# Gathering the tokens of a mixture-of-experts layer already transposed, four groups at a time

## The reference

```python
gu = jnp.einsum("td,edf->tef", h, w_expert_gu)
act = jax.nn.silu(gu[..., :EXPERT_DIM]) * gu[..., EXPERT_DIM:] * combine[..., None]
routed = jnp.einsum("tef,efd->td", act, w_expert_down)
...
x = x + gate_f * rmsnorm(f, g_post_ffn)
```

## Time and profile before

| | |
|---|---|
| median of 3 runs | 794.63 us (790.98 to 795.26) |
| the profiled execution | 798.48 us, of which the span from first to last instruction is 796.3 us |
| PE busy | 740.0 us (93% of the span) |
| DVE busy | 421.1 us (53%) |
| ACT busy | 226.0 us (28%) |
| expert weights | 64 loads of 2048 KB and 64 of 1024 KB |
| all DMA | 256.05 MB, mean 322 GB/s |

### The profile page before, as it was taken

How to read it: one execution, slowest core, us unless ns; L and a number is a source line. 1 busy time by engine, 2 the same in 40 slices (tenths; PEclk the granted TensorE clock), 3 DMA queues, 4 the chain that set the end, 5 groups by cost and what they waited for, 6 DMA issues and landing times.

```text
span 796.3 us, 12271 instructions
## 1 busy us (share of the span) xinstructions
PE 740.0 (93%) x4613; PEld 450.0 (57%) x4613; DVE 421.1 (53%) x1003; ACT 226.0 (28%) x383; POOL 85.0 (11%) x48
## 2 busy tenths in 40 slices
PE   1589999799999999999999999999999999999984
PEld 1489887687755455554544555544545555544442
DVE  3278999384366655544444445444444445544344
ACT  3225332662351122222222222222222222222132
POOL 2235554303210000000000000000000000000000
PEclk9989999989999999999999999999999999999997
DMA  9996565804595389999999999999999999999611
GB/s 322 374 363 227 212 217 206 319 1 159 143 421 204 105 323 347 367 428 426 395 430 416 357 407 427 391 424 428 377 424 419 391 428 397 362 431 422 238 55 81
DMA packets 47263, 256.05 MB, mean 322 GB/s; under 512 B 6240, under 2 KB 8896, under 8 KB 30432
## 3 DMA queue, kind: packets, MB, share of 16 engines
q1 hardware_dynamic: 39360, 247.47, 77.8%
q0 software_dynamic: 1664, 4.35, 1.8%
q10 hardware_dynamic: 6176, 3.40, 1.6%
HBM read 253.07 MB, written 2.13 MB: 320 GB/s over the span
## 4 chain that ended last, share of the span: by engine, by line
PE 76%; DMA 11%; DVE 9%; ACT 2%; issue 1%; SPq 0%; ACTq 0%; DVEq 0%
PE psum L1917 25%; PE psum L1946 10%; PE psum L1872 9%; PE psum L1889 8%; DMA w_gu<-in_w_expert_gu 7%; PE psum L498 4%; PE psum L500 3%; PE psum L499 3%; DVE psum L1026 3%; PE psum L1881 3%; PE psum L1799 3%; DMA w_gu<-in_w_in 2%; DMA w_gu<-in_w_ada 2%; PE psum L1816 1%; PE psum L1863 1%
## 5 line engine op out<-in xcount | busy, mean ns | idle before, releaser
L1917 PE MATMUL psum<-w_gu,hgT 128*32 128x512 f32 (+1 forms) x1344 | 199.7, 599 | 5.3 <-DMA w_gu<-in_w_expert_gu 4.6
L1416 DVE TENSOR_TENSOR f_acc<-f_acc,psum 128x512 f32<-128x512 f32 x168 | 115.5, 688 | 50.1 <-PE psum L1889 50.0
L1917 PEld LDWEIGHTS psum<-w_gu,hgT 128*32 128x32 f32 (+1 forms) x1344 | 61.3, 120 | 141.0 <-issue 140.1
L1946 PE MATMUL psum<-w_dn,actT 128*32 128x512 f32 (+1 forms) x672 | 102.1, 596 | 0.0
L1407 DVE TENSOR_TENSOR y_lo<-psum,y_hi 128x1024 fp32r<-128x1024 f32 x28 | 34.3, 1225 | 106.7 <-ACT y_hi L893 106.7
L1872 PE MATMUL psum<-h_hi,onehot 128*128 128x512 f32 x174 | 71.1, 409 | 0.0
L493 POOL TENSOR_TENSOR w_lo<-w_gu,w_hi 128x2048 fp32r<-128x2048 f32 x14 | 64.4, 4600 | 62.9 <-ACT w_hi L652 62.9
L1889 PE MATMUL psum<-y_hi,onehotT 128*128 128x512 f32 x168 | 70.4, 419 | 0.0
L1399 DVE SCALAR_TENSOR_TENSOR act<-sil,wsl,psum 128x256 f32<-128x256 f32 x28 | 19.0, 679 | 94.6 <-ACT sil L888 94.6
L1872 PE MATMUL psum<-h_lo,onehot 128*128 128x512 f32 x174 | 68.1, 391 | 0.0
L1889 PE MATMUL psum<-y_lo,onehotT 128*128 128x512 f32 x168 | 66.2, 394 | 0.0
(11 more groups left out here) (292 smaller groups left out, 952.7 us busy)
## 6 DMA issues: line engine op xcount, KB each, us to landing
w_gu<-in_w_expert_gu SPq DMA_DIRECT2D x64, 2048.0 KB, 13.3
w_dn<-in_w_expert_down SPq DMA_DIRECT2D x64, 1024.0 KB, 10.4
w_gu<-in_w_ada SPq DMA_DIRECT2D x12, 2048.0 KB, 16.1
w_gu<-in_w_in SPq DMA_DIRECT2D x4, 2048.0 KB, 8.5
w_gu<-in_w_out SPq DMA_DIRECT2D x2, 2048.0 KB, 10.1
bc<-mod_rows POOLq DMA_DIRECT2D x6, 512.0 KB, 7.6
w_gu<-in_w_in SPq DMA_DIRECT2D x2, 1024.0 KB, 15.5
w_gu<-in_w_shared_gu SPq DMA_DIRECT2D x1, 2048.0 KB, 9.1
```

The costliest lines, as they stand in the source:

```text
L1416: v.tensor_tensor(dst, dst, bank(5 + n), ALU.add).then_inc(f_added, 1)
L1917: ins = t.matmul(bank(2)[rows, :], hgT[:, c, rows], w_gu[s][:, c, :], start=(c == 0), stop=(c == NC - 1), tile_position=(0, rows.start))
L1946: ins = t.matmul(bank(3 + n)[rows, :], actT[:, j, rows], w_dn[s][:, j, 512 * n:512 * (n + 1)], start=(j == 0), stop=(j == 1), tile_positio ...
```

## The change

**Gather.** The operands change places: a 128x128 block of `h_hi` or `h_lo` is stationary and the one-hot matrices of four groups move, 128 tokens by 512 places. The output is the transposed activations of four groups for one chunk of 128 features, so `hg` and its transposes go. A batch is four groups, the first and the last batch two (8 batches). Each batch takes 8 chunks of 6 products. `hgT` is double and four times as wide; two chunks of the next batch are gathered in each group. The first batch is gathered before the loop, the second all in group 1.

**The one-hot matrices.** `onehot_T` goes. In its place `slots` makes three products with 6 or 8 columns for each group (routing weights and the token's number for each place), all four groups of a batch at once after the second group of the batch before; VectorE takes the results (`tokens_of`) and builds `onehotT` by comparing a row of token numbers with the token of each place.

**Order.** `combine` of a group moves one group later (in group k that of group k-1, as before), but the one with zeros in group 0 goes, with the memsets that it needed. `h_hi` and `h_lo` are written with the features in another order (reads of `hp` with a stride of 8 floats). `x` is written to DRAM (1.5 MB) before the loop, its place holds one-hot matrices, and it is read back behind the last weight load. The fixed work on the overflow table moves from before the loop to groups 3 to 5. The last products stand first in the branch for no overflow.

```diff
+BATCH = 4
+BATCHES = [list(range(0, FIXED // 2))] + [list(range(k, min(k + BATCH, GROUPS))) for k in range(FIXED // 2, GROUPS, BATCH)]
...
-            a.activation(h_hi[:, i, :], hp[:, :], ACT.Copy).then_inc(hi_ready, 1)
+            a.activation(h_hi[:, i, :, :], hp[:, :].rearrange("p (q c) -> p c q", c=NC), ACT.Copy).then_inc(hi_ready, 1)
...
+            sp.wait_ge(hgT_done, NC * NB)
+            sp.wait_ge(slots_done, GROUPS)
+            sp.dma_start(x[:, :, :], x_dram).then_inc(x_back, 16)
...
+            def onehot_T(par, ring):
+                own.wait()
+                v.tensor_scalar(onehotT[par][:, :, :], iota3[:, :, :], idx[:, ring:ring + 1], None, ALU.is_equal)\
+                    .then_inc(ohT_ready, 1)
...
+            g.wait_ge(x1_ready, NT)
+            g.dma_start(x_dram, x[:, :, :]).then_inc(x_saved, 16)
...
+            def gather(b, c, products=range(2 * NT)):
+                width = P * len(BATCHES[b])
+                if products[0] == 0 and NC * b + c >= 2:
+                    t.wait_ge(hgT_ready, NC * b + c - 1)
+                for n in products:
+                    i, part = EVERY[n]
+                    ins = t.matmul(bank(c % 2, 0, width), part[:, i, c, :], onehot[b % 2][:, i, 0:width],
+                                   start=(n == 0), stop=(n == 2 * NT - 1))
+                if products[-1] == 2 * NT - 1:
+                    ins.then_inc(hgT_done, 1)
...
+            for c in range(NC // 2):
+                gather(0, c)
             sh_down(2)
+            for c in range(NC // 2, NC):
+                gather(0, c)
...
-                    ins = t.matmul(bank(2, (P + 8) * i, (P + 8) * i + width), onehot[par][:, i, :], ident_w[:, i, 0:width],
-                                   start=True, stop=True)
-                ins.then_inc(ohT_done, 1)
+                    ins = t.matmul(bank(7, 16 * j, 16 * j + end), rows[:, i, :], weights[:, i, 0:end],
+                                   start=(i == 0), stop=(i == NT - 1))
+                ins.then_inc(slots_done, 1)
...
+                gate_up(tiles, hgT[b % 2][:, :, P * j:P * j + P], uses)
+                chunks = chunks_of(k)
+                outputs = combines(k)
+                if chunks:
+                    t.wait_ge(oh_ready, b + 2)
+                if b == 0:
+                    for m, c in chunks[:4]:
+                        gather(m, c)
+                        next(outputs, None)
+                else:
+                    for m, c in chunks:
+                        for some in (range(0, NT), range(NT, 2 * NT)):
+                            gather(m, c, some)
+                            next(outputs, None)
...
+                transposes(k + (NT + 1), act)
+                for u in range(2):
+                    next(outputs, None)
+                down(k, tiles, uses)
+                for m, c in chunks[4:]:
+                    gather(m, c)
+                if found_after(k) is not None:
+                    batch_slots(found_after(k))
...
+            with t.If(n_pairs < 1):
+                t.wait_ge(f_added, 6 * GROUPS)
+                first_totals()
+                t.wait_ge(ohT_ready, GROUPS)
+                t.wait_ge(y_ready, GROUPS)
+                all_outputs((GROUPS - 1) % 2)
             with t.Else():
```

More of the change, by code:

```diff
@@ L39 @@
 SLOTS = 4
+RING = 8
+BATCH = 4
 FIXED = 4
@@ L1354, in _ @@
             sh_a(2)
-            make_onehot(0)
+            v.wait_ge(ident_ready, NT)
+            v.wait_ge(x_saved, 16)
+            for j in range(2):
+                make_onehot(0, j)
             v.wait_ge(rank_done, 1)
@@ L1373, in _ @@
             own.link(v.tensor_tensor(part[:, :], counts, alloc[:, :], ALU.subtract))
-            for r in range(ROUNDS):
-                own.add(v.tensor_scalar(flags[:, r, :], part[:, :], float(CAP * r), None, ALU.is_gt))
-            own.wait()
-            fl = flags[:, :, :].rearrange("p r e -> p (r e)")
-            ix = index[:, :, :].rearrange("p r e -> p (r e)")
-            own.link(v.tensor_tensor_scan(ix, fl, fl, 0.0, ALU.add, ALU.bypass))
-            mt = match[:, :, :].rearrange("p r e -> p (r e)")
@@ L1801, in sh_gu, with transposes @@
                 ins.then_inc(sh_gu_done if i < NT - 1 else gu_used[s_sh], 1)
-            def transposes(count):
+            def transposes(count, src):
                 t.wait_ge(a_ready, count)
                 for j in range(2):
-                    ins = t.transpose(bank(7, P * j, P * j + P), act[:, j, :], ident)
+                    ins = t.transpose(bank(7, P * j, P * j + P), src[:, j, :], ident)
                 ins.then_inc(aT_done, 1)
+            EVERY = [(i, part) for i in range(NT) for part in (h_hi, h_lo)]
+            def gather(b, c, products=range(2 * NT)):
+                width = P * len(BATCHES[b])
+                if products[0] == 0 and NC * b + c >= 2:
[6 more added lines that the diff above has]
+                    ins.then_inc(hgT_done, 1)
             def sh_down(i):
@@ L1949, in group @@
                                 ins.then_inc(dn_used[s], 1)
[L1951 to L1967 removed]
+            batch_slots(0)
@@ L1978, in _ @@
[L1978 to L1989 removed]
+                uses = [(2 * q, loads), (2 * q + 1, loads)]
@@ new lines, in over @@
+                tiles = tiles_of([(2 * q, 0, CAP), (2 * q + 1, CAP, P)], CAP)
+                t.wait_ge(oh_ready, p + (NB + 1 - GROUPS))
+                slots(onehot_over, token_w[:, 0, 0, :, :], 0, 2)
+                t.wait_ge(hgT_ready, p * 2 + (NC * NB - 2 * GROUPS))
+                for c in range(NC):
+                    for i in range(NT):
+                        for part in (h_hi, h_lo):
+                            ins = t.matmul(bank(c // 4, P * (c % 4), P * (c % 4) + P), part[:, i, c, :], onehot_over[:, i, :],
+                                           start=(i == 0 and part is h_hi), stop=(i == NT - 1 and part is h_lo))
+                    if c % 4 == 3:
+                        ins.then_inc(hgT_done, 1)
@@ L1992, in total_so_far @@
+                t.wait_ge(y_ready, p)
+                t.wait_ge(ohT_ready, p)
+                for c in range(6):
+                    combine(jj * 2 + (GROUPS + q - 1), c, (q + 1) % 2)
+                t.wait_ge(hgT_ready, p * 2 + (NC * NB - 2 * GROUPS + 2))
+                gate_up(tiles, hgT[0][:, :, 0:P], uses)
+                transposes(p + (NT + 1), act)
+                down(p, tiles, uses)
             def total_so_far(c):
```

427 lines of the change are left out of this document (227 added, 200 removed).

## The result

The change takes 787.96 us (median of 19 runs, 782.17 to 791.45) against 793.95 us for the kernel before in the same comparison (19 runs, 789.15 to 800.8): a ratio of 0.9917, 95% interval 0.9892 to 0.9943. That is 6.6 us shorter (4.5 to 8.6), where 3.1 had been worked out. The profiled execution took 789.55 us, its span is 787.4 us.

A forecast was written before the change was run, and what follows sets the result against it. TensorE and the weight loads were taken as close to balance, loads setting the three-group cycles. +1 + 3.4 + 0.5 - 3.5 + 4 - 4.5 - 4 = -3.1 us, from a median of 794.63 to 791.5 us; range 779 to 801.

The forecast's parts named there:

- The loads set the loop's pace: Three-group cycles: loads need at least 53.9 us, TensorE alone 51.4 after the change, so nothing is won in these fifteen groups.
- rival 1: Loop loads: earlier buffer releases bring loads earlier, TensorE's saved time is really saved; -19 us, 775 us; chance 0.17 with partial forms.
- The waits: Ahead of each three-expert group: a wait for `w_gu` of 2 to 3 us, with the clock at half behind some.
- The clock: New waits ahead of groups 6, 13, 16 and 19: 60% of 1.7 us each, +4 us (0 to +7).
- Rival 2: Waits lower the clock wherever they occur, 1.7 us each: +14 in place of +4, +7 us in sum, 801 us; chance 0.21.
- what the loop gains: Steady loop: two four-group cycles -1.3 us each, group 2 gains 0.9, three-group cycles nothing; -3.5 us (0 to -19).
- The end: Groups 26 and 27 without gathers, -4.5 us (-3 to -6); closing products starting at once behind them, -4 us (-1 to -5).
- Rival 3: No net change: the end wins little as VectorE goes through its own branches, -1 in place of -4; 795 us; chance 0.12.
- Start and first groups: First gather before the loop +1 us, groups 0 and 1 together +3.4, strided writes of `h_hi` and `h_lo` +0.5.

## Why the prediction was right

**The loads set the loop's pace.** This was the first theory, with rival 1 (the landings move with the releases, 775 us) against it. Four results bear it out: the five cycles of three groups took 269.5 us after 269.6; with half the bytes the same change gave 20.6 us in place of 6.6; 19 us of work put back cost 8; and a load sent ahead of others only moved the wait. The bytes agree: seven experts of 3.15 MB are 22.0 MB a cycle, which in 53.2 us (507.60 to 560.84) are 414 GB/s, near the 424 to 437 of full windows. It is not the bytes alone. While gate/up of a three-expert group runs, no new `w_gu` is issued: behind group 13's start the next ones go out at 514.84, right behind the end of its gate/up at 514.67, and the windows from 510 to 515 and 515 to 520 us have 369 and 321 GB/s.

The waits came out otherwise than forecast. There was none ahead of group 10, 0.9 to 2.3 us ahead of five of the others, and 5.55 ahead of group 26 (2 to 3 had been said); the prediction had not seen that groups 22 to 25, which gather for a batch of two with products of 256 columns, are shorter: 15.6 us (group 24, 701.89 to 717.50) and not 16.9.

The Trainium skill, "DMA: Bandwidth & Descriptors" (Specifications), has 435 GB/s as a core's ceiling. At that figure 22.0 MB take 50.6 us, an estimate from its page, under the measured 53 to 54; the trace shows such rates only in single windows, and the sum of the prediction rightly went by the cycle's own 381 GB/s.

**The clock** had +4 us, as 60% of four cold starts of 1.7, and this term held. Two cold starts were new: gate/up of groups 16 and 19 took 8.53 and 8.63 us and not 7.0, in all 3.2 us; group 26 had its own already. That they count in full, although a load paces the loop, other traces show. The run with work put back into groups 26 and 27 has the change's own loop up to group 26, and there group 13 too began cold:

```profile
508.83 8.77 PE psum L1994 x64
...
563.97 8.57 PE psum L1994 x64
```

That is 55.1 us to group 16, against 53.2 in the change and 53.1 in the change without its closing order, where group 13 was warm. From the end of gate/up to the landing that group 16 waits for are 46.2 us against 46.0: the landing came later by as much as gate/up took longer. The other way round, the run with two chunks in group 0 had a warm group 19, and group 23 behind it:

```profile
613.55 7.07 PE psum L1993 x64
...
682.02 7.07 PE psum L1993 x64
```

That is 68.5 us, against 70.25 in the change and 70.3 to 70.5 in three other runs with a cold group 19. From group 3 to group 26 the change took 408.9 us, the change without its closing order 408.7, each with two cold starts, and the run with group 13 cold 410.4 with three. So a cold start of a three-expert group costs some 1.5 to 2 us. The releases explain it: the next `w_gu` are issued when gate/up has ended, and if it takes longer, the queue runs dry for longer (139 GB/s from 509 to 514 us behind a cold group 13 in the run with two chunks in group 0, and 369 from 510 to 515 behind the warm one in the change). Rival 2 (801 us) had this cost right and the number of such starts wrong: it took one at each place, and groups 6, 13 and 23 stayed warm.

**The term that was mis-sized** is what the loop gains. It stood at -3.5 us. From group 2 to group 26 the change was 3.2 us shorter with 3.2 us of new cold starts in it, so without them it gained 6.3. The four-group cycles gave 1.8 and 2.3 us (0.7 with group 19's cold start) where 1.3 each had been said, and group 2 0.6 (0.9). The five cycles of three groups, which were to give nothing, gave 1.6: from the end of gate/up to the landing are 46.4 us on average, 46.8 before. That their sum stayed the same to 0.1 us is partly chance, as group 16's cold start, 1.5 us, took it back. These 2.8 us and the end's below are most of the difference between the -3.1 us of the sum and the -8.9 of the spans or the -6.6 of the runs. As the range from 779 to 801 us holds both a gain and a loss, that the measured 788 lies in it says less for the prediction than these terms do.

The Trainium skill, "TensorE: Matmul & The Clock Gate" (HAM oscillation), describes a kernel in which some 2 us of products stand between waits of 3 to 5 us for loads, and each stretch of products starts cold. Here some 50 us of products stand between waits of 0.9 to 5.6 us, so the page does not say what the prediction drew from it, that all four new waits would cost. The trace has a cold start at three of the six places with a wait, and not at groups 6, 13 and 23, with 7.07 us each.

**The end.** Group 26 to the last down was worked out at 32.7 us and took 32.1; the products put back there cost 3.2 us by the trace, 5.8 (give or take 3) by the timed runs. Behind it the prediction took -4 (bounds -1 and -5); the two traces give -5.3 and the closing order alone -5.6 (3.6 to 7.7 by its interval). Mis-sized by over a microsecond: of the 3.6 us without products it was aware, of the cold clock that they caused in the closing products (4.53 us for 2.77) it was not. `y_lo`, named as the next to be late, is not: it begins at 771.77 and takes 1.22, while the six closing products end at 773.41. Rival 3 (the end wins little) fell with this.

**Start and first groups.** +3.4 and 0.5 + 1 were worked out, +3.9 and +0.7 measured, the second with a start that scatters by 3 us. Group 0 took 13.1 us (12.7 worked out) and group 1 26.6 (26.5). Writing `h_hi` and `h_lo` with the stride did take near double (2.09 to 2.17 and 2.02 us, before 1.06 and 1.22); what it costs is not shown, as the start scatters by more. Filling group 0's wait showed that 2.0 of the 3.9 us can be had.

## What to carry to other kernels

When two resources are near balance, work taken from one is worth what the other leaves: count the bytes and the products of one whole cycle before believing a saving, and a test with half the bytes tells in two runs how much is waiting to be had. A slow product in such a loop is not hidden by the wait if the next loads are issued behind it: here each cold gate/up cost its full 1.5 to 2 us. Look at the two ends of a loop, which nothing overlaps: here a reordered branch gave as much as the whole change with its rebuilt gather. A full queue is not improved by sending one load ahead of others, if what is held back leaves it dry.

## What the runs showed of the hardware

Which waits lower the clock was not what I had expected. TensorE in the changed kernel, ahead of groups 13 and 16 (idle time before, and its releaser, in brackets; the two rows of L1956 and L1994 at 558 and 560 us follow each other):

```profile
507.60 1.92 PE L1994 MATMUL psum<-w_gu,hgT 128*32 128x512 f32 x16 [1.93 <-DMA w_gu<-in_w_expert_gu]
...
558.21 1.50 PE L1956 MATMUL psum<-token_w,onehot 128*128 128x6 f32 x12
560.84 1.94 PE L1994 MATMUL psum<-w_gu,hgT 128*32 128x512 f32 x8 [1.13 <-DMA w_gu<-in_w_expert_gu]
```

and the windows there (PEclk is the third number from the end):

```profile
560.50:562.50 2.00, 1.66 (x8) 0.46 (x12) 1.72 (x14) 0.00 (x0) 0.00 (x0) 0.50 1.05 438
562.50:564.50 2.00, 2.00 (x20) 0.63 (x16) 0.00 (x0) 0.00 (x0) 0.00 (x0) 0.67 0.94 397
564.50:566.50 2.00, 2.00 (x24) 0.64 (x20) 0.00 (x0) 0.00 (x0) 0.00 (x0) 1.00 0.98 410
```

A wait of 1.93 us straight behind a product down left the clock at full (gate/up 7.07 us). One of 1.13 us behind twelve products of 6 columns in 1.50 us was followed by a granted clock of 0.50, the level of 1.2 GHz, and gate/up took 8.53. Waits of 2.32 and 5.55 us, ahead of groups 19 and 26, were followed by it too. The same place can fall either way: group 19 was warm behind 1.92 us in the run with two chunks in group 0 (7.07 us), and group 13 was cold behind 2.15 us in the run with work put back into groups 26 and 27 (8.77 us). The wait of 3.6 us ahead of the closing products lowered the clock in the kernel before (0.51), and waits of 3.4 us slowed these products in two more traces (4.33 and 4.47 us), but one of 3.40 us in the change without the new closing order did not (2.84 us, granted clock 1.00). What tells these cases apart was not tried.
